# Delta-rule stage of a hybrid decoder trunk: one projection block in TensorE's queue, split around the key products or whole behind them

## The reference

```python
def gated_delta_chunked(q, k, v, log_g, beta, s0):
    def step(s, inp):
        cum = jnp.cumsum(gi, axis=-1)
        dec = jnp.exp(jnp.where(incl, cum[..., :, None] - cum[..., None, :], -jnp.inf))
        kk = jnp.einsum('bhik,bhjk->bhij', ki, ki)
        a = jnp.where(strict, bi[..., None] * kk * dec, 0.0)
        sol = lax.linalg.triangular_solve(eye + a, rhs, left_side=True, lower=True, unit_diagonal=True)
        ...
        qk = jnp.einsum('bhik,bhjk->bhij', qi, ki) * dec
        o = jnp.einsum('bhij,bhjv->bhiv', qk, delta) + jnp.einsum('bhik,bhkv->bhiv', qi * jnp.exp(cum)[..., None], s)
```

## Time and profile before

| | |
|---|---|
| median of 3 runs | 6727.6 us (6712.52 to 6736.32) |
| the profiled execution's own time | 6737.32 us |
| its span, first to last instruction | 6735.6 us |
| PE matmul busy | 6265.5 us, 93% |
| DVE busy | 3591.6 us, 53% |
| ACT busy | 2141.3 us, 32% |
| mean granted TensorE clock | 0.958 |

### The profile page before, as it was taken

One profiled execution on the slowest core, in us unless ns is written; L12 is line 12 of the kernel. 1 busy time (PEld: TensorE's weight loads), 2 busy tenths in 40 slices (PEclk: granted clock), 3 DMA queues, 4 the chain that ended last, 5 costly groups with the idle time before them and its releaser, 6 DMA issues. The chain is left out here.

```text
span 6735.6 us, 109246 instructions
## 1 busy us (share of the span) xinstructions
PE 6265.5 (93%) x42728; PEld 5868.9 (87%) x42728; DVE 3591.6 (53%) x6661; ACT 2141.3 (32%) x3172; POOL 0.7 (0%) x6
## 2 busy tenths in 40 slices
PE   8998988979999989999989989889799999899999
PEld 6776768979999989999967767689799999899999
DVE  3444353337778865555434443533377888655554
ACT  2333333222234442222223333332222344422222
POOL 0000000000000000000000000000000000000000
PEclk9999988989999999999999999889899999999999
DMA  2212112224346655444322121122243466554543
GB/s 101 65 49 75 56 42 73 84 88 120 113 130 188 182 187 195 167 178 166 135 88 67 48 75 56 44 73 82 88 123 114 128 187 187 186 193 166 179 165 136
DMA packets 494389, 804.29 MB, mean 119 GB/s; under 512 B 81652, under 2 KB 302836, under 8 KB 475892
## 3 DMA queue, kind: packets, MB, share of 16 engines
q1 hardware_dynamic: 494116, 800.67, 37.4%
HBM read 616.20 MB, written 186.72 MB: 119 GB/s over the span
## 5 line engine op out<-in xcount | busy, mean ns | idle before, releaser
L1625 PE MATMUL ps<-xh,wh 128*128 128x288 f32 x4608 | 1376.5, 299 | 44.3 <-DVE wl L1841 44.3
L1625 PE MATMUL ps<-xl,wh 128*128 128x288 f32 x4608 | 1361.9, 296 | 0.0
L1625 PE MATMUL ps<-xh,wl 128*128 128x288 f32 x4608 | 1357.1, 295 | 0.0
L2041 PE MATMUL ps<-gh,vh 128*128 128x320 f32 (+1 forms) x4096 | 894.9, 300 | 73.2 <-DVE vl L2106 73.2
L1625 PEld LDWEIGHTS ps<-xh,wh 128*128 128x128 f32 x4608 | 867.2, 188 | 47.5 <-DVE wl L1841 45.2
L2041 PE MATMUL ps<-gl,vh 128*128 128x320 f32 (+1 forms) x4096 | 884.6, 298 | 0.0
L2041 PE MATMUL ps<-gh,vl 128*128 128x320 f32 (+1 forms) x4096 | 884.3, 297 | 0.0
L1625 PEld LDWEIGHTS ps<-xh,wl 128*128 128x128 f32 x4608 | 868.4, 188 | 0.0
L1625 PEld LDWEIGHTS ps<-xl,wh 128*128 128x128 f32 x4608 | 867.2, 188 | 0.0
L2106 DVE TENSOR_TENSOR vl<-vr,vh 128x512 fp32r<-128x512 f32 x512 | 353.2, 690 | 690.3 <-ACT vh L2061 690.0
L2041 PEld LDWEIGHTS ps<-gh,vh 128*128 128x128 f32 x4096 | 634.6, 191 | 86.2 <-issue 74.3
(11 more groups left out here) (374 smaller groups left out, 9175.7 us busy)
## 6 DMA issues: line engine op xcount, KB each, us to landing
raw<-in_u SPq DMA_DIRECT2D x256, 512.0 KB, 4.0
vr<-in_v SPq DMA_DIRECT2D x512, 256.0 KB, 2.9
activated<-go SPq DMA_DIRECT2D x256, 288.0 KB, 4.3
coefficients<-wt SPq DMA_DIRECT2D x36, 2048.0 KB, 9.3
gb<-activated SPq DMA_DIRECT2D x64, 1152.0 KB, 5.9
wb<-coefficients SPq DMA_DIRECT2D x64, 1152.0 KB, 8.3
wr<-in_w_cm SPq DMA_DIRECT2D x104, 512.0 KB, 4.5
wm<-in_w_merge SPq DMA_DIRECT2D x32, 768.0 KB, 4.2
```

What stands on the lines that cost most here:

```text
L1625: last = nc.tensor.matmul(out, wp[:, slot, k, :], xp[:, k, cols], start=(k == 0 and wp is T.wh and xp is T.xh), stop=(k == KD - 1 and wp i ...
L2041: last = nc.tensor.matmul(out, vp[:, x % 4, m * P:(m + 1) * P], gp[:, row, col:col + size], start=begins, stop=False, skip_group_check=True)
```

## The change

Block 2 is no longer cut in two. All 8 matmuls stand behind the key products; `ahead(2)` is `ahead(2, 0, 8)`, with the same waits at its head.

```diff
             last.then_inc(s["betab_done"], 1)
-            ahead(2, 0, 4)
             pe.wait_ge(s["qk_ready"], 1)
             scores(0, k, range(TILES))
-            ahead(2, 4, 4)
+            ahead(2)
             pe.wait_ge(s["r1_ready"], 1)
```

## The result

The changed kernel takes 6742.9 us (median of 20 runs), the kernel before 6727.94 (20 runs, 6712.52 to 6737.88). Of the changed kernel's runs 19 lie at 6729.21 to 6754.06 and one, slow at a mean granted clock of 0.825, took 7164.78. The ratio is 1.0022, with a 95% interval of 1.0015 to 1.0029. On another chip it was 6743.24 against 6724.4, a ratio of 1.0024 (1.0016 to 1.0033). So the change costs 15 to 19 us, where 8.7 were forecast. That is the forecast direction and inside its range of 6719 to 6753, but about twice the amount.

What follows compares the result with a forecast made beforehand. PE bounds the whole (93% busy), but DVE's chain sets when the solve can begin. Six clock falls of 1.5 us (9.0), less 0.65, plus 0.4 for delays, give +8.7 on 6727.6: 6736 us, range 6719 to 6753.

Steps and rivals of the forecast that it cites:

- The first half leaves its place: Before the key products: they start 0.36 us earlier, PE gets 1.58 us of new idle time, and DVE's L1061 gains nothing.
- The block behind them, and the queue: Behind the key products: the whole block ends at 200.77, L805 starts 0.68 us later, the solve 0 to 0.1 us later.
- The term of 0.4 us for the eight stages: At the solve's start in each delta-rule stage: a delay of 0.05 us, 8 x 0.05 = 0.4 us.
- The clock: Over the key products and the block: granted clock falls in most stages, 6 of 8 taken, 1.5 us each; chance 0.56.
- Its size: In the delta-rule stages: 6 falls at 1.5 us, 9.0 us, less 0.65 already lost in the seventh stage.
- falls in most stages: Likeliest case, in the delta-rule stages: three to eight falls at 0.65 to 1.7 us, +2 to +14 us; chance 0.56.
- the slower rival: At the solve's chain: clock still at 0.50, a second stretch paid in all eight stages, 24 us, 6752; chance 0.11.
- No fall: In the delta-rule stages: clock stays at 1.00, PE's slack takes up the rest, +0.4 us, 6728; chance 0.28.
- The faster one: In the last head's stages: clock comes back earlier, -4 us in each of two stages, 6720; chance 0.05.

Runs made afterwards that it cites:

- the block-first kernel: Against the changed kernel, block 2 stands whole ahead of the key products instead of behind them; 6726.23 us, ratio 0.9989 to the kernel before.
- the one with DVE's early scaling: Against the changed kernel, DVE's scaling of k moved ahead of its five subtractions of the decay matrix; 6753.8 us, ratio 1.0041 to the kernel before.
- the version with block 3 fed: Against the kernel before, the first of block 3's eight matmuls moved ahead of the solve; 6718.69 us, ratio 0.9991, and again 6716.67, ratio 0.9987.

## Why the prediction was right, and where it was short

**The first half leaves its place.** Forecast: key products at 195.77 in the first stage, 2.78 us behind L828, after 1.58 us without work. Measured: 2.77. (The 1.42 us of idle time are counted from the end of L828; the 1.58 from where the next matmul could have started, 0.16 us sooner.) They bring DVE nothing, as said: its L1061 (1060 after) starts at 5.37 us behind L828 before and at 5.39 after.

**The block behind them, and the queue.** Forecast: L805 late by 0.68 us, the solve by 0 to 0.1. With the clock at full, measured 0.78 and 0.00 (the kernel with wide products in the gap and the one with them among the narrow products). The slack before L805 and before the solve takes it all. The term of 0.4 us for the eight stages was nothing.

**The clock.** This carried the forecast and is shown. The fall is there in all eight stages in two profiles. With wide products in the gap it is gone in six of them, and in the other two it begins sooner. With narrow ones in the gap it is there in all eight. It is gone in all eight when the narrow products ahead of the gap are broken up while the gap stays. But the new idle time is not the cause of all of it: in two stages of the first profile and three of the second the fall begins ahead of the gap, behind the narrow products, and the gap accounts only for its second half. The rule of the Trainium skill (TensorE: Matmul & The Clock Gate, section "Why this matters for your kernels"), whose advice on drops in mid-kernel names long idle gaps only, does not decide here. The same gap of 1.42 us stood in the changed kernel, where the clock fell in all eight stages, and in the one with the narrow products broken up, where it fell in none; and with no gap at all, but narrow products, it fell in all eight.

**Its size** is where the sum was short. I took 6 falls of 1.5 us. There were 8, and two of them lasted twice as long. By the start of the solve they cost six times 1.45 to 1.60 and twice 2.46 us, 14.0 in all. Less the 0.65 that the seventh stage had lost before, and less 2.0, since in the two long cases the fall at the stage's beginning was missing, this is 11.3 us, where the forecast had 8.4. (L828 comes 14.06 us behind the barrier in those two stages and 15.06 in the others.) The stages' sums agree: +9.2, with 2.0 us on the other side, in the sixth stage of the execution before, where the solve started at 11.39 behind L828 at full clock because DVE was late.

**The rest**, 4 to 8 us of the 15 to 19, is the difference between these 11.3 us and the medians, and so lies outside the delta-rule stages. The two profiles show no place for it: in both, the six attention stages with a next head are longer (5.8 and 5.7 us) and the last two shorter (6.0 and 3.2), and the profile of before is of an execution 9.7 us slower than its median. The clock of the timed executions tells more. Its mean was 0.9556 over the changed kernel's second twelve and 0.9593 over the 29 of the kernel before in the same runs. That is about 50 us more at 1.2 GHz (an estimate: 2 x 0.0037 x 6730), and the traces show 26 us more of it in the delta-rule stages. So clock lost elsewhere fits the rest; where, and whether by the shift, is open. The forecast costed unedited stages at nothing, and that step was wrong.

The same record sorts the other runs. Over the 86 recorded executions of the kernel before, 0.001 more of mean clock goes with 5.4 us less (a fitted line, an estimate, which misses single executions by 2.8 us). Held against this line, the block-first kernel is 7 us above, the one with DVE's early scaling 6, the one with the narrow products broken up 10, near the 9, 6 and 12 us of their local delays. The changed kernel is 4 us below it, so its loss goes with the clock. Differences of 4 us and less, that of the version with block 3 fed among them, are too small to be read this way.

**The range.** The forecast's own width for falls in most stages was +2 to +14 us. The measured 15 to 19 lies above it; it is inside the range because of what was added for the scatter of few runs and for the slower rival. The 20 us that the forecast took as the limit of what can be told from none was too much: with 20 runs of each kernel the interval of the ratio is 1.0015 to 1.0029.

**The rivals.** No fall is refuted. The slower one, a clock still low when the chain of the solve begins, did not happen: the long falls of two stages began sooner, and the clock was back at 1.00 more than 3 us before the solve. The faster one forecast 4 us in each last head. There the delta-rule and attention stages together took 147.6 and 147.9 us before and 146.7 and 146.6 after, though the new fall cost 1.6 in each; in the second profile it is 146.7 and 147.9. A gain of some 2.5 us in a stage may be there, but with one profile of before it can't be told from scatter.

## What to carry to other kernels

A block of wide matmuls ahead of a wait can be worth more than its own time, because it keeps PE computing in a stretch that would otherwise lose the clock; even one of eight was enough here. Look for stretches of narrow products next to a wait, since the busy share calls them busy, and read the granted clock right behind them. Costs and gains of a few microseconds must be judged by the stage as well as by the total, because unedited stages of one kind differed by up to 15.5 us in sum between these kernels. Stages are best cut at their barriers, and the mean granted clock of each timed execution belongs beside its time.

## What the runs showed of the hardware that was not expected

- Between two orders that differ by one matmul of 0.49 us the falls go from all to none: 8 of 8 stages with 1.42 us of idle time behind the narrow products and L828, 0 of 8 with that matmul and 0.93 us of idle time.
- A fall can begin with no idle time ahead of it: in the second stage of the changed kernel as L828 ends, and in the first stage of the kernel with wide products in the gap.
- PE work that computes something can cost less than nothing: 24 wide matmuls added, their results thrown away, made the changed kernel 18 us faster, by the medians of different chips.
- A narrow product is no help: 56 of them, one column each, in place of the idle time gave 6751 us, and in three stages some 10 us at 1.2 GHz from the start of L828 on.
- Executions of one kernel differ in their mean granted clock, and their times with it: the 86 of the kernel before run from 6701.81 us at 0.963 to 6741.17 at 0.956.
